# An encoder kernel: modulation sums turned into columns on TensorE, their weight tiles read by sixths and in another order

## The chip, the cores and the metric

The kernel runs on one core of a Trainium2 chip. The metric is the device time of one execution in microseconds (us). Three runs of the kernel before took 875.2, 884.22 and 884.54 us (median 884.22). The profiled execution took 870.41 us.

## The reference

The kernel computes a trunk of two residual layers over 256 tokens of width 1024, in float32. What matters here is the modulation: each layer takes six vectors of 1024 from a conditioning vector, and uses them at different places.

```python
c_act = jax.nn.silu(c)
for l in range(2):
    mod = c_act @ ada_w[l] + ada_b[l]           # (1024) @ (1024, 6144)
    sh1, sc1, g1, sh2, sc2, g2 = jnp.split(mod[:, None, :], 6, axis=-1)
    h = _rmsnorm(x, norm_mix_g[l]) * (1.0 + sc1) + sh1
    # l = 0: z = h @ even_w_in; gated linear recurrence + neighbourhood attention; mixed = [..] @ even_w_out
    # l = 1: z = h @ odd_w_in;  dilated attention + pooling;                      mixed = [..] @ odd_w_out
    x = x + g1 * mixed
    h = _rmsnorm(x, norm_ffn_g[l]) * (1.0 + sc2) + sh2
    x = x + g2 * _conv_ffn(h, ffn_w_up[l], ffn_conv_w[l], ffn_conv_b[l], ffn_w_down[l])
return _rmsnorm(x, final_norm_g)
```

## The kernel before

All activations are feature-major (128 partitions are features, 256 tokens are columns). Projection weights come in **units** of 128x2048 float32 (1 MB). Each unit is read by SyncE (SP) into one of four buffers `w_raw`, rounded by ScalarE (ACT) into `w_hi` (`split_hi`, L474), subtracted by VectorE (DVE) into `w_lo` (`split_lo`, L704), and used by TensorE (PE) in 48 matmuls (`three`, L1049). `w_hi` and `w_lo` have two buffers (SPLIT = 2): `w_hi` of unit n+2 waits until PE is done with unit n. There are 110 units, in order: EI (16, input projection of layer 0), EO (4, its output projection), UP0 (22) and DN0 (11) (feed-forward), OI (20), OO (4), UP1 (22), DN1 (11).

Beside these, DVE computes `c_act @ ada_w`. A tile of 128 rows (k) by 1024 columns (q) is read into one of two buffers `ada_raw`; DVE multiplies it by `cact[:, k]` and adds it into `mod_acc` (`add_tile`, L714). The partition sum that is left is made on PE: `mod_sum` (L1112) runs one matmul for each 128 columns, with a one-hot picker as the stationary operand and `mod_acc` as the moving one, so that group g lands in row g; DVE copies the rows out (`keep_mods`, L719), PE transposes them (`mod_turn`, L1119), and DVE adds the bias (`take_mods`, L724). The first 2048 columns of layer 0 are summed in eight tiles at the start (L771, L774). The other 80 tiles follow in the order k outside, q inside, so that a group of 2048 or 4096 columns is complete only at its end; `mod_acc` is cleared by POOL (GpSimd) before each group.

Every engine runs its own list in program order and waits on semaphores. Where the 80 tiles stand on DVE: 20 beside EI (one for each of units 0 to 7, two for each of 8 to 12, one for 13 and 14), 9 in the neighbourhood attention (after each odd step of `attend`, 16 steps), 3 in the recurrence after it, 16 beside the first 16 units of UP0, 24 beside OI (two for each of its first four units, then one), 8 in the dilated attention (odd steps from 3 on). POOL loads the tiles (`tile_in`, L391: it waits until the buffer's tile is used, then issues), except those in the two attentions, which SP loads (L364, L375). After its first 20 tiles POOL computes the gates of the recurrence (L421 to L431).

In `attend` PE computes the scores of step s (L1201 or L1318 and L1323), transposes those of step s-2 (L1178) and multiplies by the values for step s-3 (L1206, or L1330 and L1333); DVE adds the bias and takes the maximum (L848 or L858, L840, L841), ACT takes the exponential (L552) and copies the transposes out (L559).

`norm` on DVE takes the reciprocal (L735), then per feature block a product (L747) and, after ACT's rounding (L495), the rest `h_lo` (L754). The update of x after DN0 is eight instructions on DVE (L983); ACT squares them (L483), PE sums (L1101). In the last unit of DN0 `down_summed` already tells DVE which blocks of x can be updated.

Of the kernel before, what the change touches and what calls it, by code (L numbers as in the profile page):

```python
# [14 lines left out]
P = 128  # L15
# [25 lines left out]
ADA1, ADA2, ADA3, ADAS = 8, 40, 56, 88  # L41
# [13 lines left out]
C_PICK = C_EPS + 1  # L55
C_HMEAN = C_PICK + 63
# [24 lines left out]
def shape_constants():  # L81
# [32 lines left out]
    a[:, C_PICK + 31] = 1.0  # L114
# [5 lines left out]
def encoder(nc, x, c, ada_w, ada_b, norm_mix_g, norm_ffn_g, even_w_in, even_w_out, hgrn_lb_logits, hgrn_norm_g,  # L120
            na_rpb, odd_w_in, odd_w_out, pool_w, pool_scale, ffn_w_up, ffn_conv_w, ffn_conv_b, ffn_w_down,
            final_norm_g, consts_in, out):
    with ExitStack() as ctx:
# [31 lines left out]
        mod_rows = sb("mod_rows", [32, P])  # L155
# [80 lines left out]
        rest_landed = [sem(f"rest_landed{i}") for i in range(2)]  # L236
        ada_used, acc_zeroed, mod_summed, mod_ready = sem("ada_used"), sem("acc_zeroed"), sem("mod_summed"), sem("mod_ready")
# [20 lines left out]
        down_summed, mod_gathered, mod_kept = sem("down_summed"), sem("mod_gathered"), sem("mod_kept")  # L258
# [38 lines left out]
        def _(sp):  # L297
# [63 lines left out]
            for tile in range(20, 32):  # L361
                sp.wait_ge(ada_used, ADA1 + tile - 1)
                k, q, slot = tile // 4, tile % 4, tile % 2
                sp.dma_start(ada_raw[:, slot, :], ada_w[0, k * P:(k + 1) * P, 2048 + q * 1024:3072 + q * 1024]).then_inc(  # L364
                    rest_landed[slot], 16)
# [6 lines left out]
            for tile in range(24, 32):  # L372
                sp.wait_ge(ada_used, ADA3 + tile - 1)
                k, q, slot = (tile - 16) // 2, 2 + tile % 2, tile % 2
                sp.dma_start(ada_raw[:, slot, :], ada_w[1, k * P:(k + 1) * P, 2048 + q * 1024:3072 + q * 1024]).then_inc(  # L375
                    rest_landed[slot], 16)
# [9 lines left out]
        def _(pool):  # L386
            def tile_in(l, k, q, slot, i2, t2):

                pool.wait_ge(ada_used, i2 * 2 + 2 * t2 + slot - 1)
                src = ada_w[l].rearrange("(k p) n -> k p n", p=P)[bass.ds(k, 1), :, q:q + 1024]  # L390
                pool.dma_start(ada_raw[:, slot, :], src.rearrange("k p n -> p (k n)")).then_inc(ada_landed[slot], 16)  # L391

            def head(l, base):
                tile_in(l, 0, 0, 0, 0, base // 2)
                tile_in(l, 0, 1024, 1, 0, base // 2)
                with pool.Fori(1, KT) as k:
                    for q in (0, 1):
                        tile_in(l, k, q * 1024, q, k, base // 2)
# [289 lines left out]
        def _(dve):  # L688
# [18 lines left out]
            def add_tile(k, q, slot, i2, t2, landed=ada_landed, before=ADA1):  # L707

                dve.wait_ge(ada_used, i2 * 2 + 2 * t2 + slot - 1)
                if before == ADA1 and t2 >= ADA2 // 2:  # L710
                    before += 12
# [680 lines left out]
```

## Time and profile before

| | |
|---|---|
| profiled execution, its time | 870.41 us |
| its span (first to last instruction) | 868.7 us |
| median of three runs | 884.22 us (875.2 to 884.54) |
| TensorE busy | 797.4 us (92%) |
| VectorE busy | 599.5 us (69%) |
| ScalarE busy | 422.8 us (49%) |
| GpSimd busy | 71.7 us (8%) |
| DMA | 171.17 MB, mean 197 GB/s |

Times in the rows are microseconds from the span's start unless marked ns. Busy shares are averages over stages with different limits, so each stage is read by itself. "PE" is the matmul, "PEld" the load of its stationary operand, which overlaps it. An arrow "<-" after a time names what ended the idle time before it. "PEclk" is the clock that TensorE was granted: 1.00 is 2.4 GHz, 0.50 is 1.2 GHz.

### The profile page before, as it was taken

To read this page: it belongs to the slowest core of one execution; us is meant where nothing else is said; L and a number is where in the kernel's file an instruction comes from. 1 tells how busy PE (TensorE), PEld (TensorE's weight loads), DVE (VectorE), ACT (ScalarE), POOL (GpSimd) and SP (SyncE) were. 2 spreads that over 40 slices of the span, in tenths; PEclk is the share of its full clock that TensorE was granted. 3 is DMA by queue.
4 is the path that set the end of the run, shared out by engine and by line. 5 is a ranking of instruction groups with operands and counts; after the bars stand their busy time and mean duration, and the time that the engine had idled before them with its cause. 6 is when DMAs were issued, how large, how long until landed. Compare 5 with 4: busy or idle time off the path is not lost.

```text
span 868.7 us, 17243 instructions
## 1 busy us (share of the span) xinstructions
PE 797.4 (92%) x6580; PEld 750.3 (86%) x6580; DVE 599.5 (69%) x870; ACT 422.8 (49%) x664; POOL 71.7 (8%) x89
## 2 busy tenths in 40 slices
PE   3399998986898999999989999999998999999996
PEld 2299996675788999999979899977787999999995
DVE  3876687779759999874466766667735777776444
ACT  4244464331246666663345444634344666666332
POOL 0200117000200000000020100050000000000000
PEclk9699998577899999999999999995579999999998
DMA  9999885322364999755563898852505576765511
GB/s 360 332 261 330 295 287 194 98 73 81 116 175 122 289 289 290 221 198 207 185 224 134 296 308 296 279 170 76 144 3 146 144 194 193 193 194 194 193 49 48
DMA packets 160047, 171.17 MB, mean 197 GB/s; under 512 B 5178, under 2 KB 142339, under 8 KB 158979
## 3 DMA queue, kind: packets, MB, share of 16 engines
q1 hardware_dynamic: 151363, 139.11, 51.0%
q0 software_dynamic: 8640, 31.46, 10.2%
q8 instruction: 29, 0.48, 0.2%
q14 instruction: 15, 0.12, 0.0%
HBM read 169.50 MB, written 1.05 MB: 196 GB/s over the span
## 4 chain that ended last, share of the span: by engine, by line
PE 79%; DVE 12%; DMA 5%; issue 2%; ACT 1%; SPq 1%; POOLq 0%; DVEq 0%; ACTq 0%
PE acc L1049 50%; PE big L1049 14%; DMA ada_raw<-in_ada_w 4%; PE aux L1178 2%; DVE mod_acc L774 2%; DVE mod_acc L714 2%; DVE qk L287 2%; PE big L1318 2%; PE aux L1101 1%; PE big L1201 1%; PE acc L1206 1%; PE acc L1330 1%; DVE w_lo L704 1%; PE big L1323 1%; PE acc L1112 1%
## 5 line engine op out<-in xcount | busy, mean ns | idle before, releaser
L1049 PE MATMUL acc<-h_hi,w_hi 128*128 128x256 f32 x1248 | 351.4, 282 | 17.3 <-DVE h_lo L754 14.8
L1049 PE MATMUL acc<-h_lo,w_hi 128*128 128x256 f32 x1248 | 348.6, 279 | 0.0
L1049 PE MATMUL acc<-h_hi,w_lo 128*128 128x256 f32 x1248 | 348.6, 279 | 0.0
L704 DVE TENSOR_TENSOR w_lo<-w_raw,w_hi 128x1024 fp32r<-128x1024 f32 x220 | 263.1, 1221 | 105.0 <-ACT w_hi L474 104.9
L474 ACT ACTIVATE w_hi<-w_raw 128x1024 fp32r<-128x1024 f32 x220 | 224.5, 1050 | 101.3 <-PE big L1049 62.4
L1049 PEld LDWEIGHTS acc<-h_hi,w_hi 128*128 128x128 f32 x1248 | 238.4, 191 | 19.6 <-issue 17.7
L1049 PEld LDWEIGHTS acc<-h_lo,w_hi 128*128 128x128 f32 x1248 | 238.1, 191 | 0.4
L1049 PEld LDWEIGHTS acc<-h_hi,w_lo 128*128 128x128 f32 x1248 | 237.8, 191 | 0.0
L714 DVE SCALAR_TENSOR_TENSOR mod_acc<-ada_raw,cact,mod_acc 128x1024 f32<-128x1024 f32 x80 | 106.8, 1338 | 21.8 <-DMA ada_raw<-in_ada_w 21.6
L1049 PE MATMUL big<-hid_hi,w_hi 128*128 (+1 forms) x352 | 97.2, 276 | 0.0
L1049 PE MATMUL big<-hid_lo,w_hi 128*128 (+1 forms) x352 | 97.2, 276 | 0.0
L1049 PE MATMUL big<-hid_hi,w_lo 128*128 (+1 forms) x352 | 97.2, 276 | 0.0
L1049 PEld LDWEIGHTS big<-hid_hi,w_lo 128*128 128x128 f32 x352 | 66.1, 188 | 0.0
L1049 PEld LDWEIGHTS big<-hid_hi,w_hi 128*128 128x128 f32 x352 | 66.1, 188 | 0.0
L1049 PEld LDWEIGHTS big<-hid_lo,w_hi 128*128 128x128 f32 x352 | 66.1, 188 | 0.0
L391 POOL DMA_DIRECT2D ada_raw<-in_ada_w x60 | 32.1, 535 | 287.3 <-DVE mod_acc L714 287.3
L610 ACT ACTIVATE conv<-acc,vecs 128x256 f32<-128x256 f32 x44 | 24.9, 565 | 59.2 <-PE acc L1049 58.5
L952 DVE SCALAR_TENSOR_TENSOR conv<-acc,vecs,conv 128x255 f32<-128x255 f32 x44 | 21.2, 483 | 39.3 <-ACT conv L610 37.5
L1049 PE MATMUL acc<-w_hi,h_hi 128*128 128x256 f32 x144 | 40.0, 278 | 0.7 <-DVE w_lo L704 0.7
L1049 PE MATMUL acc<-w_hi,h_lo 128*128 128x256 f32 x144 | 39.8, 277 | 0.0
L1049 PE MATMUL acc<-w_lo,h_hi 128*128 128x256 f32 x144 | 39.8, 277 | 0.0
L523 ACT ACTIVATE ze<-acc 128x512 f32 (+1 forms) x16 | 9.6, 598 | 47.5 <-PE acc L1049 47.5
(184 smaller groups left out, 911.8 us busy)
## 6 DMA issues: line engine op xcount, KB each, us to landing
w_raw<-in_ffn_w_up SPq DMA_DIRECT2D x88, 512.0 KB, 5.0
ada_raw<-in_ada_w POOLq DMA_DIRECT2D x60, 512.0 KB, 5.6
w_raw<-in_ffn_w_down SPq DMA_DIRECT2D x44, 512.0 KB, 4.0
w_raw<-in_odd_w_in SPq DMA_DIRECT2D x40, 512.0 KB, 5.0
w_raw<-in_even_w_in SPq DMA_DIRECT2D x32, 512.0 KB, 6.0
ada_raw<-in_ada_w SPq DMA_DIRECT2D x20, 512.0 KB, 3.8
ada_first<-in_ada_w SPq DMA_DIRECT2D x5, 1024.0 KB, 8.1
w_raw<-in_even_w_out SPq DMA_DIRECT2D x8, 512.0 KB, 5.2
```

The lines of the kernel that those rows point to most:

```text
L287: return eng.tensor_tensor(to, to, total.unsqueeze(3).to_broadcast([P, 2, half // (2 * h), h]), ALU.mult)
L391: pool.dma_start(ada_raw[:, slot, :], src.rearrange("k p n -> p (k n)")).then_inc(ada_landed[slot], 16)
L474: nc.scalar.activation(w_hi[:, n % SPLIT, part], w_raw[:, n % RAW, part], ACT.Copy).then_inc(s_hi, 1)
L523: nc.scalar.activation(to, acc[:, (n - first) % 2, :], ACT.Copy, scale=scale).then_inc(z_evicted, 1)
L610: nc.scalar.activation(conv[:, a, :], acc[:, a, 0:T], ACT.Identity, bias=vecs[:, bass.ds(i * 4 + (V_CB + l * FT + u), 1)], scale=vecs[:, b ...
L704: dve.tensor_tensor(w_lo[:, n % SPLIT, part], w_raw[:, n % RAW, part], w_hi[:, n % SPLIT, part].bitcast(F32), ALU.subtract).then_inc(s_lo, 1)
L714: dve.scalar_tensor_tensor(out=sums, in0=ada_raw[:, slot, :], scalar=cact[:, bass.ds(k, 1)], in1=sums, op0=ALU.mult, op1=ALU.add).then_inc ...
L774: dve.scalar_tensor_tensor(out=sums, in0=ada_first[k], scalar=cact[:, k:k + 1], in1=sums, op0=ALU.mult, op1=ALU.add).then_inc(ada_used, 1)
L952: dve.scalar_tensor_tensor(out=conv[:, a, 1:T], in0=acc[:, a, 0:T - 1], scalar=tap(0), in1=conv[:, a, 1:T], op0=ALU.mult, op1=ALU.add).the ...
L1049: ins = pe.matmul(dst, lhsT, rhs, start=start and n == 0, stop=stop and n == 2, skip_group_check=True)
L1178: ins = pe.transpose(aux[:, r % 2, j * P:(j + 1) * P], (ns if base == 0 else cs)[:, r % 4, j * P:(j + 1) * P], ident)
L1318: pe.matmul(bank[:, 0:T], rows(0, 0, t * P, P), rows(6, 0, 0, T), start=True, stop=True)
```

## The change

`mod_sum`, `keep_mods` and `mod_turn` go, with the picker, `mod_rows` and the clearing of `mod_acc`. In their place PE takes `mod_acc` as the stationary operand and one column of ones as the moving one, once for each 128 columns, and DVE adds the bias to what stands in PSUM. The tiles are taken a sixth (1024 columns) at a time, all eight k of it, and each sixth is turned into columns shortly before its use. POOL loads all 80 tiles; its loops and DVE's are written out.

```diff
+ADA_FIRST = 8
+ADA_TILES = [(0, q, k) for q in (2, 3, 4, 5) for k in range(KT)] + [(1, q, k) for q in range(6) for k in range(KT)]
+ADA_AT = {(0, 2): 0, (0, 3): 1, (0, 4): 2, (0, 5): 3, (1, 0): 0, (1, 1): 1, (1, 2): 2, (1, 3): 3, (1, 4): 0, (1, 5): 1}
+def ada_summed(l, q):
+    return ADA_FIRST + ADA_TILES.index((l, q, KT - 1)) + 1
 ...
@@ sync: the loads of the tiles in both attentions go
-            for tile in range(20, 32):
-                sp.wait_ge(ada_used, ADA1 + tile - 1)
-                ...
-            for tile in range(24, 32):
-                ...
@@ gpsimd
+            def load_tiles(first, last):
+                for tile in range(first, last):
+                    l, q, k = ADA_TILES[tile]
+                    pool.wait_ge(ada_used, ADA_FIRST + tile - 1 if tile >= 2 else 6)
+                    pool.dma_start(ada_raw[:, tile % 2, :], ada_w[l, k * P:(k + 1) * P, q * 1024:(q + 1) * 1024]).then_inc(
+                        ada_landed[tile % 2], 16)
-            pool.wait_ge(mod_gathered, 1)
-            pool.memset(mod_acc[:], 0.0).then_inc(acc_zeroed, 1)
-            rest(0, ADA1, 0, 5)
+            load_tiles(0, 20)
             pool.wait_ge(lb_ready, 1)
 ...         (the gates, L421 to L428)
             pool.tensor_tensor(qk[:, 2, :], qT, fT[0], ALU.mult).then_inc(gates_ready, 1)
+            load_tiles(20, 22)
             pool.wait_ge(z_evicted, N_EI)
             pool.tensor_tensor(own_k, qk[:, 0, :], qk[:, 3, :], ALU.add).then_inc(own_ready, 1)
-            ...
+            load_tiles(22, 72)
 ...         (the pooling, L448 to L458)
+            load_tiles(72, 80)
@@ scalar
-                stream(act, first_down, N_DN, 4, lambda i, n: split_hi(i, n + SPLIT)) if l == 0 else \
-                    stream(act, first_down, N_DN - SPLIT, 4, lambda i, n: split_hi(i, n + SPLIT))
+                stream(act, first_down, N_DN - 1 if l == 0 else N_DN - SPLIT, 4, lambda i, n: split_hi(i, n + SPLIT))
 ...
             rms(2)
+            split_hi(0, OI + 1)
             norm(2, mods[:, 1, 0:8])
@@ vector
+            def add_tiles(first, last):
+                for tile in range(first, last):
+                    l, q, k = ADA_TILES[tile]
+                    sums = mod_acc[:, ADA_AT[l, q] * 1024:(ADA_AT[l, q] + 1) * 1024]
+                    dve.wait_ge(ada_landed[tile % 2], (tile // 2 + 1) * 16)
+                    if k == 0:
+                        dve.tensor_scalar(sums, ada_raw[:, tile % 2, :], cact[:, 0:1], None, ALU.mult).then_inc(ada_used, 1)
+                        continue
+                    dve.wait_ge(ada_used, ADA_FIRST + tile)
+                    dve.scalar_tensor_tensor(out=sums, in0=ada_raw[:, tile % 2, :], scalar=cact[:, k:k + 1], in1=sums,
+                                             op0=ALU.mult, op1=ALU.add).then_inc(ada_used, 1)
@@ norm: the fourth norm takes its shift and gain first
                 if idx:
                     reciprocal_rms(idx)
+                if idx == 3:
+                    take_mods(5, 1, 24, 16, aux[:, 1])
+                    make_gain(3, 1, 32, V_NFFN + KT)
@@ EI: the same places as before (20 tiles)
+            in_units(EI, EI + 8, 0, 1)
+            in_units(EI + 8, EI + 10, 8, 2)
 ...
@@ neighbourhood attention: 4 tiles, after steps 3, 7, 11, 15
-                if s < STEPS + 2 and s % 2:
-                    add_rest(20 + s // 2)
+                if s % 4 == 3 and s < STEPS:
+                    add_tiles(20 + s // 4, 21 + s // 4)
@@ recurrence: 3 tiles go
-            add_rest(29)
-            add_rest(30)
-            add_rest(31)
-            keep_mods(1, 32, big[:, 0])
+            take_mods(1, 0, 16, 24, big[:, 0])
@@ UP0 16 tiles, DN0 1 and then 2 for each unit, DN1; UP1 8 tiles
+                    for u in range(N_UP):
+                        up_step((24 + u, 25 + u) if u < 16 else (0, 0))(0, first_up + u)
+                    split_lo(0, first_down + SPLIT)
+                    add_tiles(40, 41)
+                    take_mods(2, 0, 40, 8, aux[:, 1])
+                    for u in range(1, N_DN - 1):
+                        split_lo(0, first_down + u + SPLIT)
+                        add_tiles(39 + 2 * u, 41 + 2 * u)
                 else:
+                    for u in range(N_UP):
+                        up_step((72 + u // 2, 73 + u // 2) if u < 16 and u % 2 else (0, 0))(0, first_up + u)
+                    split_lo(0, first_down + SPLIT)
+                    take_mods(6, 1, 40, 8, aux[:, 1])
+                    stream(dve, first_down + 1, N_DN - SPLIT - 1, 4, lambda i, n: split_lo(i, n + SPLIT))
@@ OI: 13 tiles, one for each of units 0 to 12
+            split_lo(0, OI + 1)
+            in_units(OI, OI + 13, 59, 1)
+            in_units(OI + 13, OI + N_OI, 72, 0)
@@ dilated attention: 8 tiles go; keep_mods and the second half of the rows go
-                if s == 2:
-                    keep_mods(3, 32, acc[:, 1])
 ...
+            take_mods(4, 1, 16, 8, aux[:, 1])
@@ tensor
+            def mod_columns(tiles, first, count, bank):
+                pe.wait_ge(ada_used, tiles)
+                for g in range(count):
+                    at0 = (first + g) % 32 * P
+                    ins = pe.matmul(bank[:, g:g + 1], mod_acc[:, at0:at0 + P], consts[:, C_ONE:C_ONE + 1], start=True,
+                                    stop=True)
+                ins.then_inc(mod_summed, 1)
+            mod_columns(ADA_FIRST, 0, 16, aux[:, 1])                           # before EI
+            mod_columns(ada_summed(0, 4), 0, 24, big[:, 0])                    # before EO
+                mod_columns(ada_summed(1, 4), 8 * ADA_AT[1, 3], 16, aux[:, 1]) # before UP1, after norm_sum_of(3)
+                mod_columns(ada_summed(l, 5), 8 * ADA_AT[l, 5], 8, aux[:, 1])  # between UP and DN, both layers
+            mod_columns(ada_summed(1, 1), 0, 16, aux[:, 1])                    # after DN0
+            mod_columns(ada_summed(1, 2), 8 * ADA_AT[1, 2], 8, aux[:, 1])      # before OO
-            attend(STEPS, ROW, dil_scores, dil_values, cpt, ctok, N_EI + N_OI, half_mods)
+            attend(STEPS, ROW, dil_scores, dil_values, cpt, ctok, N_EI + N_OI)
```

## Rows read from the trace of the kernel before

**Rows 1.** The page's busy digits in 40 slices of 21.7 us; PEclk is TensorE's granted clock.

```profile
PE   3399998986898999999989999999998999999996
PEclk9699998577899999999999999995579999999998
```

**Rows 2.** Table by stage: us, busy us and count of PE, PEld, DVE, ACT, POOL, clock, DMA.

```profile
138.00:182.00 44.00, 39.67 (x136) 27.18 (x134) 36.04 (x90) 17.09 (x57) 13.32 (x9) 0.56 0.34 104
572.00:634.00 62.00, 60.47 (x379) 44.20 (x377) 45.71 (x126) 25.54 (x61) 13.78 (x11) 0.62 0.36 103
```

**Rows 3.** Timeline of POOL after its first tiles: start, us, engine, line, operation.

```profile
143.56 2.35 POOL L428 TENSOR_TENSOR qk<-ze 128x1024 f32<-128x1024 f32 x1
145.87 3.33 POOL L429 TENSOR_TENSOR qk<-ze 128x1024 f32<-128x1024 f32 x1
```

**Rows 4.** Timeline of DVE in the neighbourhood attention: a tile, steps 4 and 16.

```profile
143.67 3.32 DVE L714 SCALAR_TENSOR_TENSOR mod_acc<-ada_raw,cact,mod_acc 128x1024 f32<-128x1024 f32 x1
146.91 0.15 DVE L829 RECIPROCAL stat<-stat 128x1 f32<-128x1 f32 x1
177.87 0.15 DVE L829 RECIPROCAL stat<-stat 128x1 f32<-128x1 f32 x1
```

**Rows 5.** Timeline around the first unit of EO.

```profile
222.12 7.17 PE L1112 MATMUL big<-mod_acc,consts 128*32 128x128 f32 x64
231.62 0.24 PE L1119 MATMUL big<-consts,mod_rows 32*128 32x32 f32 x1 [2.33 <-DVE mod_rows L719]
232.38 1.23 DVE L762 TENSOR_TENSOR h_lo<-work,h_hi 128x1024 fp32r<-128x1024 f32 x1 [0.81 <-ACT h_hi L590]
```

**Rows 6.** The chain of work that ended last: DN0, OI's first unit, OI's last 13 units.

```profile
384.97 59.85 PE big L1049 x528
...
457.32 7.33 PE acc L1049 x48
...
500.76 71.43 PE acc L1049 x624
```

**Rows 7.** Timeline of DVE after DN0: the updates of x, directly behind `w_lo`.

```profile
448.22 3.22 DVE L983 SCALAR_TENSOR_TENSOR xT<-big,mods,xT 128x256 f32<-128x256 f32 x8
```

**Rows 8.** Timeline of DVE in OI beside two tiles a unit.

```profile
471.69 2.36 DVE L704 TENSOR_TENSOR w_lo<-w_raw,w_hi 128x1024 fp32r<-128x1024 f32 x2 [0.62 <-ACT w_hi L474]
498.28 2.35 DVE L704 TENSOR_TENSOR w_lo<-w_raw,w_hi 128x1024 fp32r<-128x1024 f32 x2
```

**Rows 9.** DMA issues, KB each, median us to landing: tiles in UP0, weights in DN0.

```profile
ada_raw<-in_ada_w POOLq DMA_DIRECT2D x16, 512.0 KB, 6.3
w_raw<-in_ffn_w_down SPq DMA_DIRECT2D x12, 512.0 KB, 3.7
```

**Rows 10.** Timeline of weight loads and the sums, in the dilated attention.

```profile
575.16 3.68 PE L1112 MATMUL acc<-mod_acc,consts 128*32 128x128 f32 x32
580.54 0.52 PEld L1330 LDWEIGHTS acc<-zo,cpt 128*128 128x128 f32 x4
589.25 0.98 PEld L1330 LDWEIGHTS acc<-zo,cpt 128*128 128x128 f32 x4
```

**Rows 11.** Windows of 2 us (columns as in Rows 2) where the clock falls.

```profile
142.00:144.00 2.00, 0.20 (x1) 0.23 (x2) 1.86 (x7) 1.10 (x4) 1.92 (x3) 0.92 0.53 111
584.00:586.00 2.00, 1.55 (x15) 0.91 (x13) 1.90 (x9) 0.81 (x3) 1.84 (x3) 1.00 0.77 209
```

**Rows 12.** Timeline of PE: scores of steps 6 and 15, and what ends the stage.

```profile
587.17 1.03 PE L1318 MATMUL big<-zo 64*128 64x256 f32 x2
622.92 1.22 PE L1318 MATMUL big<-zo 64*128 64x256 f32 x2
633.99 3.64 PE L1351 MATMUL big<-pmean,poolw 128*128 128x256 f32 x8
```

**Rows 13.** Timeline of the norm before UP1: the last sums and DVE's reciprocal.

```profile
667.09 1.13 PE L1101 MATMUL aux<-squared,consts 128*128 128x256 f32 x4 [0.16 <-ACT squared L483]
668.76 1.75 DVE L735 RECIPROCAL rstd<-rstd 128x256 f32<-128x256 f32 x1 [1.79 <-ACT rstd L488]
```

More of the change, by code:

```diff
@@ L386, in _ @@
         def _(pool):
[L387 to L398, printed above, removed]
-            def rest(l, base, first=0, last=KT):
-                with pool.Fori(first, last) as k:
-                    for q in range(4):
-                        tile_in(l, k, 2048 + q * 1024, q % 2, k * 2, base // 2 + q // 2)
+            def load_tiles(first, last):
[4 more added lines that the diff above has]
+                        ada_landed[tile % 2], 16)
             done = [0]
@@ L785, in _, with in_units @@
             dve.tensor_tensor(lbt[:, 0, :], logits, logits, ALU.subtract).then_inc(lb_diff, 1)
-            dve.wait_ge(acc_zeroed, 1)
-            def in_step(first, base, tile0, per):
-                def step(i, n):
-                    if not (isinstance(i, int) and n + SPLIT in (EO, EO + 1, OO, OO + 1)):
-                        split_lo(i, n + SPLIT)
-                    for tile in range(tile0 + per * (n - first), tile0 + per * (n - first + 1)):
-                        add_tile(i * per + tile // 4, tile % 4, tile % 2, i * 2 * per, base // 2 + tile // 2)
-                return step
+            def in_units(first, last, tile, per):
+                for n in range(first, last):
+                    if n + SPLIT not in (EO, EO + 1, OO, OO + 1):
+                        split_lo(0, n + SPLIT)
+                    add_tiles(tile + per * (n - first), tile + per * (n - first + 1))
             def keep_bias(first, last):
@@ L1104, in norm_sum_of @@
                     ins.then_inc(norm_sum, 1)
-            def mod_sum(e, tiles, count, bank, first=0, last=None):
+            def mod_columns(tiles, first, count, bank):
                 pe.wait_ge(ada_used, tiles)
-                last = count if last is None else last
-                for g in range(first, last):
-                    pick = consts[:, C_PICK + 31 - g:C_PICK + 31 - g + count]
-                    ins = pe.matmul(bank[0:count, 0:P], pick, mod_acc[:, g * P:(g + 1) * P], start=g == first,
-                                    stop=g == last - 1)
-                ins.then_inc(mod_gathered, 1)
-            def mod_turn(e, count, bank):
-                pe.wait_ge(mod_kept, e + 1 + (e == 3))
-                pe.transpose(bank[:, P:P + count], mod_rows[0:count, :], ident[0:count, 0:count]).then_inc(mod_summed, 1)
+                for g in range(count):
[3 more added lines that the diff above has]
+                ins.then_inc(mod_summed, 1)
             pe.wait_ge(s_ident, 16)
```

111 lines of the change are left out of this document (14 added, 97 removed).

## The prediction

> **What bounds the kernel now.** I read the page's digits first. PE is busy nearly everywhere, but its granted clock falls in two places, slices 6 to 10 and 31 to 33 [rows 1]. The table by stage says which: the neighbourhood attention at a mean clock of 0.56 and the dilated attention at 0.62; elsewhere PE streams units at 59.85/11 = 5.44 us each [rows 2, 6]. So a change outside PE counts only where it makes PE wait, adds to PE's list, or moves the point at which the clock falls. The tiles do this in three ways: DVE is in program order, so a tile that has not landed holds back `w_lo` or a step of attention behind it; POOL loads tiles and computes, in order too; and DVE's tile time in the attentions opens gaps on PE. The sums at 222 to 229 are hidden beside the reciprocals of the recurrence; those after step 2 of the dilated attention are not.
>
> **Price of a column.** Before, 16 groups took 3.68 us at full clock [rows 10]. After, each is a full 128x128 weight load, recorded twice for float32, and one moving column. No row has one moving column. Nearest is L1330, 128x128 loads with 64 moving columns: four in 0.52 us, one every 0.11 after the first (0.19), and 0.98 at half clock, one every 0.21 [rows 10]. I take 0.22 us a group at full clock: 8 groups 1.75, 16 groups 3.5, 24 groups 5.3. The lower end is nothing at all, since a single moving column may need no wait for the load before; the upper is 0.43, both loads at half clock. So PSUM columns cost what rows cost; the gain is only the copy and the transpose.
>
> The Trainium skill, TensorE: Matmul & The Clock Gate, section Back-to-back issue gap, lists matmuls of 1 to 64 columns at about 60 cycles, a floor of about 25 ns. Read alone it would make 16 groups 0.8 us; an estimate by that page. Rival D below is what this would do here, priced from the rows.
>
> **Part by part**, each against the profiled execution (870.41 us, span 868.7; the median of the runs is 13.8 us above it).
>
> 1. *Start.* 16 groups at half clock cost at most 16 x 0.43 = 6.9 us instead of 6.3; copy and transpose (0.6) go. Zero, bounds +0.6 and -3. Clearing `mod_acc` is off the path. EI has its 20 tiles at the same places: zero.
>
> 2. *Neighbourhood attention: +6.5.* Nine tiles of 1.28 us become four, which gains nothing by itself: from step 4 at 146.91 to step 16 at 177.87 the cadence is 2.58 us and the mean clock is half [rows 2, 4]. But tile 20 changes queue. SP issued it before the stage began; now POOL issues it behind the gates. The last two products there start at 143.56 (2.35) and 145.87 (3.33 beside DVE's stretched tile; 2.35 without it), so the issue comes at 148.2 [rows 3]. It lands 3.7 us later at best (weights of the same size in the quieter DN0) and 6.3 at worst (tiles in UP0) [rows 9]; I take 4.2, as nothing else is read here. DVE wants this tile after step 3, at about 142.5, since the tile after step 1 is gone. It stands until 152.4, and step 4 starts at 153.7 instead of 146.91: +6.8, less 0.4 for the second stretched tile that goes. Behind that wait stand all steps, so PE idles about 8 us; the clock fell after a shorter gap (0.20 busy in 2 us [rows 11]) and stays down. Bounds +5.5 and +9.
>
>    That tile took 3.32 us and POOL's product 3.33 side by side [rows 3, 4]. The Trainium skill, SBUF — State Buffer, says that the port pair that VectorE and GpSimd share is an exclusive lock, against a VectorE instruction with two SBUF inputs too. By it the product takes 2.35 when DVE stands; without it the term would be 1 us larger.
>
> 3. *Recurrence and EO: -2.* Three tiles leave DVE where it had time. PE's 24 groups end at 222.1 + 5.3 = 227.4, and no transpose makes it wait for DVE until 231.62: the first half of EO's first unit (24 matmuls, 2.7 us) runs before `h_lo`, which ends at 233.6 [rows 5]. Gain 2.8 at full clock, 1 if the wait brings the clock down. I take 2.
>
> 4. *UP0.* 16 tiles as before, zero. Eight groups between UP0 and DN0, 1.75 us, are in the next sum.
>
> 5. *DN0: +7.* It had no tiles; now 19, two beside each unit from the second on. The row with two tiles a unit is OI's start: `w_lo` at 471.69 and, four units later, at 498.28, a cadence of 6.65 us against PE's 5.44 [rows 8]. A buffer's round is its use, POOL's issue and the landing. From DN0's start: PE ends unit 0 at 7.2, and `w_lo` of unit n+2 is done 3.4 to 3.5 after unit n (the last one ended at 448.2, PE at 444.8) [rows 6, 7]. Units 2 to 4 get theirs at 10.7, 16.1, 21.5, still by PE's pace; unit 5 at 27.3. Six cadences on, OI's first has it at 67.2, its two tiles end 4.3 later, less 1.2 as two tiles only multiply: 70.3. There the updates of x begin, where they began at 448.22 - 384.97 = 63.25. The moved `split` of OI's second unit (ACT 2 us, DVE 2.36) is in that difference; it now sits behind the norm, where ACT has the reciprocal's 1.75 us as cover and DVE ends it 0.2 us after PE needs it. Bounds: landings of 3.7 bring DVE's round under PE's pace and the updates to about 62 (-1); those of 6.3 in UP0 [rows 9] a cadence of 7.9 and 79 to 80 (+16).
>
> 6. *OI: -3.3.* Thirteen single tiles fit 5.44 us (2.36 + 1.28). Seven units took 500.76 - 457.32 = 43.4 us against 38.1; 1.9 of the excess is the first unit's (7.33), the rest goes [rows 6]. Bounds -4, -2.5.
>
> 7. *Dilated attention: -4.* 16 groups leave PE's list after step 2 (3.6), and DVE's tiles there, but the clock falls about as early. PE had been busy 1.55 of 2 us before step 6 at 587; from there steps take (622.92 - 587.17)/9 = 3.97 us [rows 11, 12]. DVE's tiles are gone, yet ACT's `split_hi` at step 4 (2 us) and DVE's `split_lo` at step 8 (2.36) remain, each a gap on PE. Bounds: -2.5, and rival A.
>
> 8. *Before OO: -1.* 8 groups for 16 and a transpose less, but PE then waits for `h_lo`, and the clock may rise later. Bounds +0.6, -2.3.
>
> 9. *Norm before UP1: +1.5.* 16 groups start at 668.2 and end 3.5 later, at 671.7; DVE's reciprocal ended at 670.5 and its products began. Bias and gain (0.4) come after: products at 672.1, +1.6. PE is idle less, and the clock may hold: bounds 0, +1.9 [rows 13].
>
> 10. *UP1 to DN1: +1.75*; the 8 tiles of UP1 fit as UP0's 16 do.
>
> Sum: 0 + 6.5 - 2 + 7 - 3.3 - 4 - 1 + 1.5 + 1.75 = **+6.5 us**: 876.9 against the profiled execution, 890.7 against the median. The four times of before lie at 870.4, 875.2, 884.2 and 884.5, and nothing here says which kind of execution comes next; I put the time between these two, nearer the median: 886.
>
> **Rivals.**
>
> *A: the clock holds in the dilated attention* (0.25). Half of 3.97 is 1.99; with handovers that don't scale I take 2.4 us a step. Steps 6 to 15 gain 1.6 each (16), the last part, 622.92 to 633.99, gives 5, and the two splits cost 5: term 7 is -20. Term 8, now at full clock, is -3. Total -11.5, faster. For it: PE at full clock up to 586 even beside tiles and POOL; against: the splits, one of which ran when the clock fell. If it holds only to step 9, the total is +1.
>
> *B: DN0 is paced by landings* (0.2). Beyond a cadence of 7.0 us the kernel is over 1% slower. A landing of 5.3 makes it 7.2 and the total +10.5; the 6.3 of UP0 makes it 7.9 and the total +16. For: 2 MB a unit on the DMA engines, twice what DN0 had. Against: weights in DN0 land in 3.7, half that of tiles in UP0 [rows 9].
>
> *C: tile 20 is not late* (0.1): POOL lets it out before the gates end, or DVE comes later. Then no gap at 143: total 0, or -10 if the clock also stays up.
>
> *D: a group costs nothing but its issue* (0.1): terms 9 and 10 and 1.75 of term 5 go, total +2.
>
> *The forecast* has 0.35.
>
> A measurement of this kernel can tell about 1% (8.8 us) from no change. Faster by over 1%: A in most of its share, half of C: 0.23. Slower by over 1%: B, and the forecast with its DN0 term above 9: 0.32. The rest 0.45. Range: A on a quick execution is 859, on the median 872.7; B on the median 895 to 900. I leave out the outer parts: 866 to 900. The forecast's own range is 874 to 895.
>
> **What would show it.** DVE idle 8 to 11 us before a tile after step 3, released by the DMA; `w_lo` every 6.65 us in DN0 and PE waiting for it; the updates of x 70 us after DN0's start; no wait for tiles in OI; the clock's fall at step 5 to 8 of the dilated attention; groups of 0.22 us. I am wrong if tile 20 lands before 146, if DN0 stays at 60 to 62 us, or if the clock stays up past step 12.

## The result, and the profile after

The kernel after takes 919.93 us (median of 4 runs, 915.35 to 921.37) against 879.71 (4 runs beside it): a ratio of 1.053, with a 95% interval of 1.045 to 1.062. It is slower by some 40 us, where I had forecast 886 us with 900 as the upper end. The profiled executions stand at 920.08 and 870.41 us.

The table by stage of the kernel after, first for the neighbourhood attention, then for the stretch that holds the start of the dilated attention (columns as in [rows 2]; line numbers are those of the kernel after):

```profile
141.00:191.00 50.00, 39.37 (x134) 26.89 (x132) 26.62 (x85) 16.46 (x56) 15.07 (x15) 0.52 0.23 71
604.00:606.00 2.00, 2.00 (x17) 1.19 (x15) 0.36 (x2) 1.45 (x2) 0.33 (x1) 1.00 0.00 0
606.00:608.00 2.00, 1.53 (x19) 0.93 (x18) 1.90 (x9) 1.62 (x3) 1.85 (x3) 0.91 0.00 0
608.00:610.00 2.00, 1.99 (x6) 1.01 (x6) 1.93 (x6) 0.71 (x2) 1.92 (x2) 0.50 0.00 0
```

Then the chain of waits of the kernel after: start, us, what. These are the long pieces of PE, in the order of EI, UP0, OI, UP1, and the last two with the columns of the modulation before them.

```profile
41.27 59.22 PE acc L994 x480
...
270.36 129.66 PE acc L994 x1056
...
487.11 117.39 PE acc L994 x960
...
709.64 128.62 PE acc L994 x1056
...
838.26 1.68 PE aux L1056 x16
839.95 63.46 PE big L994 x528
```

The last row is the one to read. DN1 has no tiles, no waits and no edit but the columns ahead of it; its 528 matmuls are those of [rows 6], where DN0 took 59.85 us (DN1 took 59.84). Now they take 63.46. UP0 went from 121.45 us to 129.66 for 1,056 matmuls, and UP1 from 121.54 to 128.62. Streamed matmuls have become slower in stages that the change doesn't touch. The timeline shows it one by one (start, us, engine, line):

```profile
290.06 0.28 PE L994 MATMUL acc<-h_hi,w_hi 128*128 128x256 f32 x1
290.18 0.28 PE L994 MATMUL acc<-h_lo,w_hi 128*128 128x256 f32 x1
290.30 0.28 PE L994 MATMUL acc<-h_hi,w_lo 128*128 128x256 f32 x1
290.42 0.28 PE L994 MATMUL acc<-h_hi,w_hi 128*128 128x256 f32 x1
290.54 0.28 PE L994 MATMUL acc<-h_lo,w_hi 128*128 128x256 f32 x1
```

One start every 0.12 us. I took the distances between the starts of all matmuls of this kind (5,280 in each kernel; those of 108 to 130 ns, over 5,100 of them, which leaves out waits, changes of stage and the stretches at half clock) and found three values and little else: in before 113.3 ns, and 117.8 in some stretches; in after 120.0 ns, always. The mean above 113.33 ns, times 5,280, I call the **pace's part**: 2.4 us in before, 35.1 in after. Without it the spans are 866.3 and 883.2 us: +16.9. So some 33 of the 49.6 us are a pace that no term of the prediction contains, and 17 stand against the predicted 6.5. The split is an estimate: it takes PE to be the limit everywhere, which it isn't in DN0 (below), and it holds against the profiled execution of before, a quick one with one matmul in ten at 117.8.

What the change does to the layout is easy to miss in the diff. The picks in the constants shrink from 63 columns to one and `mod_rows` goes: 704 bytes less. Buffers are placed one behind another, so `h_hi`, `h_lo` and the arena (with `hid_hi`, `hid_lo`) move down by 704 bytes in each partition, while `w_hi` and `w_lo` stay. From `w_hi` to `h_hi` it is 88 KiB and 704 bytes in before, 88 KiB exactly in after.

### The profile page after: what moved, and what is told of

Its sections match the earlier page's. It is cut to its first block, busy times and chain, and to the rows that moved or that the text cites. A ratio compares the mean times of both kernels' runs of the same rounds, so it can differ in the third digit from the quotient of the medians.

```text
span 918.3 us, 16610 instructions
## 1 busy us (share of the span) xinstructions
PE 842.4 (92%) x6576; PEld 797.4 (87%) x6576; DVE 589.9 (64%) x868; ACT 422.4 (46%) x664; POOL 68.8 (7%) x106
## 4 chain that ended last, share of the span: by engine, by line
PE 80%; DVE 8%; DMA 6%; issue 2%; ACT 2%; POOL 1%; SPq 1%; DVEq 0%; ACTq 0%; POOLq 0%
PE acc L994 55%; PE big L994 8%; DMA ada_raw<-in_ada_w 5%; PE aux L1116 2%; PE aux L1056 2%; DVE mod_acc L749 2%; DVE qk L291 2%; PE big L1258 2%; PE aux L1046 2%; DVE mod_acc L690 1%; PE acc L1270 1%; PE big L1139 1%; PE acc L1144 1%; PE big L1263 1%; PE big L1056 1%
## 5 line engine op out<-in xcount | busy, mean ns | idle before, releaser
L994 PE MATMUL acc<-h_hi,w_hi 128*128 128x256 f32 x1248 | 361.3, 289 | 13.2 <-DVE h_lo L729 13.2
L994 PE MATMUL acc<-h_lo,w_hi 128*128 128x256 f32 x1248 | 359.0, 288 | 0.0
L994 PE MATMUL acc<-h_hi,w_lo 128*128 128x256 f32 x1248 | 358.6, 287 | 0.0
L447 ACT ACTIVATE w_hi<-w_raw 128x1024 fp32r<-128x1024 f32 x220 | 224.2, 1049 | 114.4 <-PE big L994 71.7
L994 PEld LDWEIGHTS acc<-h_hi,w_hi 128*128 128x128 f32 x1248 | 245.8, 197 | 14.4 <-issue 14.0
L994 PEld LDWEIGHTS acc<-h_lo,w_hi 128*128 128x128 f32 x1248 | 245.8, 197 | 0.4
L994 PEld LDWEIGHTS acc<-h_hi,w_lo 128*128 128x128 f32 x1248 | 245.6, 197 | 0.0
L690 DVE SCALAR_TENSOR_TENSOR mod_acc<-ada_raw,cact,mod_acc 128x1024 f32<-128x1024 f32 x70 | 89.7, 1281 | 37.3 <-DMA ada_raw<-in_ada_w 36.6
L994 PE MATMUL big<-hid_hi,w_hi 128*128 (+1 forms) x352 | 100.2, 285 | 3.2 <-DVE w_lo L677 3.2
L386 POOL DMA_DIRECT2D ada_raw<-in_ada_w x80 | 42.8, 535 | 662.5 <-DVE mod_acc L690 346.1
L915 DVE SCALAR_TENSOR_TENSOR conv<-acc,vecs,conv 128x255 f32<-128x255 f32 x44 | 21.2, 483 | 50.7 <-ACT conv L583 50.7
L1056 PEld LDWEIGHTS aux<-consts,mod_acc 128*128 128x128 f32 x144 | 22.0, 241 | 13.2 <-DVE mod_acc L749 12.9
```

What stands on the lines that cost most here:

```text
L386: pool.dma_start(ada_raw[:, tile % 2, :], ada_w[l, k * P:(k + 1) * P, q * 1024:(q + 1) * 1024]).then_inc(ada_landed[tile % 2], 16)
L447: nc.scalar.activation(w_hi[:, n % SPLIT, part], w_raw[:, n % RAW, part], ACT.Copy).then_inc(s_hi, 1)
L690: dve.scalar_tensor_tensor(out=sums, in0=ada_raw[:, tile % 2, :], scalar=cact[:, k:k + 1], in1=sums, op0=ALU.mult, op1=ALU.add).then_inc(a ...
L915: dve.scalar_tensor_tensor(out=conv[:, a, 1:T], in0=acc[:, a, 0:T - 1], scalar=tap(0), in1=conv[:, a, 1:T], op0=ALU.mult, op1=ALU.add).the ...
L994: ins = pe.matmul(dst, lhsT, rhs, start=start and n == 0, stop=stop and n == 2, skip_group_check=True)
L1056: ins = pe.matmul(bank[:, g:g + 1], mod_acc[:, at0:at0 + P], consts[:, C_ONE:C_ONE + 1], start=True, stop=True)
```

## The experiments

**First group: the layout, and the late tile.** pad704 puts back the lost 704 bytes and keeps the change.

```diff
+        place[0] += 704
         h_at = place[0]
```

> The changed kernel with 704 bytes left free ahead of h_hi, so that h_hi, h_lo and all that follows stand at the addresses they have in the kernel before (the shorter constants and the missing mod_rows had moved them down by 704 bytes). Nothing else differs. Placement theory (the stationary and the moving operand's addresses set the pace of float32r matmuls): 48 matmuls of a unit take 5.44 to 5.5 us again instead of 5.77 to 5.9, the 110 units save 36 us, time about 883 us. Code theory (written-out loops, instruction reads or the mix on other engines slow PE): pace stays at 0.120 us a matmul, 919 us.

Measured: 893.45 us (4 runs), 1.012 [1.006, 1.019] of before; the profiled span 896.9. Some stages are at 113.3 ns, others at 117.8, none at 120.0. That is 26 us off the 919.93 of after, and 10 us above the 883 that I expected: the stretches at 117.8 were in no expectation of mine.

before320 does the reverse: the kernel before, with 320 bytes more ahead of `h_hi`, which makes the distance 89 KiB exactly.

> The kernel before with 320 bytes left free ahead of h_hi, so that h_hi has the same place within 1024 bytes as in the changed kernel. Placement theory: units slow from 5.44 to 5.77 us, +36 us, about 906 to 916 us. Code theory: 870 to 884 us as before.

Measured: 900.27 us (2 runs), 1.021 [1.013, 1.030] of before. Nothing of the change is in it, and its pace is 120.0 ns throughout. From its chain:

```profile
822.59 63.36 PE big L1050 x528
```

That shows that the layout alone does it, and that it does not need the change. The median is 20 us above that of before beside it (880.04), and not the 26 to 36 that were expected: the profiled execution of before had few stretches at 117.8, and others at its distance have more (below). So against medians the layout explains 20 to 26 of the 40 us, and 33 of 49.6 only against the quick profiled execution. pad64 is after with 64 bytes more.

> The changed kernel with h_hi and all behind it 64 bytes higher. If the place within 128 bytes decides (before: 64, after: 0, and w_hi and w_lo at 0), the pace is 0.113 us a matmul and the time about 883 us. If the place within 256 bytes or more decides, or only the exact address before is good, it stays near 919 us. Code theory: 919 us.

Measured: 906.2 us (1 run); 113.3 or 117.8 ns by stretches, mostly the latter: neither 883 nor 919.

pad704_early is pad704 with `load_tiles(0, 22)` ahead of POOL's gates, and no `load_tiles(20, 22)` behind them.

> As pad704, and POOL loads tiles 20 and 21 before it computes the gates. Queue theory (DVE's 9.6 us wait after step 3 is POOL's order): the wait for the DMA goes, step 4 starts some 7 to 9 us earlier, against pad704 -8 us, and up to -15 if the clock then holds longer. Rival (the stage is bound by PE at half clock and something else is late next, ACT or POOL's gates themselves): under 3 us.

Measured: 878.6 and 891.9 us; the trace is that of the first. Its timeline of POOL has the request ahead of the gates, and DVE waits 0.22 us for the tile after step 3 where after has 9.63:

```profile
135.61 0.53 POOL L387 DMA_DIRECT2D ada_raw<-in_ada_w  x1 [0.95 <-DVE mod_acc L690]
136.27 3.01 POOL L404 TENSOR_SCALAR ze<-ze,lbt 128x512 f32<-128x512 f32 x4
```

```profile
141.63 1.28 DVE L690 SCALAR_TENSOR_TENSOR mod_acc<-ada_raw,cact,mod_acc 128x1024 f32<-128x1024 f32 x1 [0.22 <-DMA ada_raw<-in_ada_w]
```

EO starts at 224.4 us where pad704 has 235.7. Of these 11.3 us, 8.6 are in the attention itself (42.1 us from EI's last matmul to the first one of the recurrence, for 50.7), 1.0 in EI, which the edit doesn't touch, and 1.7 between the attention and EO.

**Second group: which property of the layout.** The parts are h against w, h alone, the bytes moved, and the unit.

```diff
-        place = [(nc.sbuf_base + 63) // 64 * 64]
+        place = [(nc.sbuf_base + 63) // 64 * 64 + 64]   # base64, base64_h64
...
+        place[0] += 64                                   # base64_h64 (pad128: 128, pad32: 32)
         h_at = place[0]
```

> The kernel after, with h_hi, h_lo and all behind them moved up by 128 bytes (h_hi at byte 139520 of a partition, 0 modulo 128, like w_hi at 49280). Theory, parity: the pace of a float32r matmul hangs on whether the addresses of h and of w stand in the same half of a 128-byte line. Here they do again, as in after and before320, so all 5,280 matmuls go at 120.0 ns and the profiled span is 915 to 920 us (883 and the pace's 35). Rival, distance: what counts is how near the layout is to that of before (pad64 906, pad704 893): then 128 bytes give at most what 64 gave, some 903 to 908 us, at a mean of 117 to 118 ns.

> The kernel after, with every buffer, w_hi and w_lo too, moved up by 64 bytes (w_hi at 49344, h_hi at 139456, both 64 modulo 128). Theory, relative: w and h in the same half of a 128-byte line means 120.0 ns throughout, 915 to 920 us. Rival, absolute: it is the place of h alone that counts; with h at 64 modulo 128 the pace is 113.3 or 117.8 ns by stretches as in pad64, 890 to 907 us.

> The kernel after, with every buffer moved up by 64 bytes and h_hi, h_lo and all behind them by another 64 (w_hi at 49344, 64 modulo 128; h_hi at 139520, 0 modulo 128). Theory, relative: w and h stand in different halves of a 128-byte line, so 113.3 or 117.8 ns by stretches, 890 to 907 us. Rival, absolute: h at 0 modulo 128 means 120.0 ns throughout, 915 to 920 us.

> The kernel after, with h_hi, h_lo and all behind them moved up by 32 bytes (h_hi at 139424, 32 modulo 128; w_hi at 49280, 0 modulo 128). If the unit is a half line of 64 bytes, h still begins in w's half: 120.0 ns, 915 to 920 us. If each 32 bytes counts, the pace is another one: 113.3 ns throughout would give 883 to 888 us, and a value between gives 895 to 907 us.

Measured, one run each: 912.12, 920.11, 907.39 and 900.00 us. base64 goes at 120.0 ns throughout and base64_h64 at 113.3 or 117.8: the distance between the two operands decides, not the place of h. pad128 is at 118.7 and pad32 at 117.1 ns, so both of my rules failed: neither "half lines of 128 bytes" (which wanted 120.0 for both) nor "the nearer to before the better". Only the loosest expectation, a value between the two for pad32, was met.

**Third group: what is left without the pace.** spread is pad704 with the later tiles one to a unit:

```diff
+                    tile = 41
                     for u in range(1, N_DN - 1):
                         split_lo(0, first_down + u + SPLIT)
-                        add_tiles(39 + 2 * u, 41 + 2 * u)
+                        more = 2 if u in (2, 5) else 1
+                        add_tiles(tile, tile + more)
+                        tile += more
...
-            in_units(OI, OI + 13, 59, 1)
-            in_units(OI + 13, OI + N_OI, 72, 0)
+            in_units(OI, OI + N_OI, 52, 1)
```

> The kernel pad704 with one edit: in the first down projection DVE adds tiles 40 to 51 (one with each unit, two with units 2 and 5) and not 40 to 56 or so with two in each unit; tiles 52 to 71 go one with each unit of the odd input projection. Theory, landings: the chain of pad704 shows a wait for ada_raw of 4.2 to 6.8 us in each unit of that projection, with two tiles to a unit. With one tile it is the matmuls (48 by 113.3 ns, 5.44 us a unit) again, so the stage from its columns to the first matmul of the odd input projection takes 74 to 77 us where pad704 takes 86, and the span less the pace's part is 872 to 876 (pad704: 884.5). Rival, something else paces it (the w_down landing, a DVE that has three more things to do): 83 us or more in the stage and 881 to 885 in all.

> pad704 with both edits: tiles 20 and 21 are requested by POOL before the gates (as in pad704_early) and the later tiles are spread (as in spread). Theory: the two gains are in different stages and add up. pad704_early has 871.1 us less the pace's part, spread takes another 9 to 11 off: 860 to 863, and with a pace's part of 5 to 12 a span of 866 to 875, 868 to 878 us: equal to the kernel before or 1% faster. Rival, the gain of one stage is lost in the next (the odd input projection with 20 tiles takes 3 to 5 us more): 873 to 882, not faster than before.

> early_spread with 32 matmuls of the identity by itself (128x128, into an unused part of two banks) in steps 0 and 1 of the dilated attention, where the kernel before had the 32 matmuls that sum the modulation; the result of them is not used. Theory, clock: the work that left these steps had kept the clock at full, which fell 3.3 us into the stage in after and about 15 us into it in before; with the fill it falls 8 us or more later, the steps until then run at full clock and win back what the fill costs (3.5 us): the stage takes 68 to 70.5 us, as without it. Rival: the fall has nothing to do with what PE does in these steps; it comes as early, and the stage takes 3.5 us more, 72 to 73 us.

> The kernel after with h_hi, h_lo and all behind them moved up by 96 bytes (h_hi 96 bytes above w_hi, modulo 256). Runs so far, by the distance from w_hi to h_hi modulo 256: 0 bytes 120.0 ns, 32 bytes 117.1, 64 bytes 113.3 or 117.8 by stretches, 128 bytes 118.7, 192 bytes 113.3 or 117.8 by stretches. Theory, a smooth function with its floor between 64 and 192 is already against the 128 bytes; by a rule of half lines 96 bytes lies as 64 and 32 together: 115 to 117.8 ns, a span of 893 to 906 us. Rival: 96 gives 113.3 throughout, 883 to 887 us.

spread: 889.3 us. DN0 from its columns to OI's first matmul takes 78.8 us, 76.4 without the pace's part; pad704 has 86.3 and 85.8. The whole gained less: the span without the pace's part is 881.2, for 884.5 of pad704, and 872 to 876 had been expected. The dilated attention gave back 3.5 us (71.9 for 68.4, from OI's last matmul to OO's first), beside a clock that was down for 71.7 us and not 61.4; why it was is not shown. For DN0 the chain of waits says why. This is DN0 in the kernel after, a round of which is a landing, an addition and an issue:

```profile
418.37 5.36 DMA ada_raw<-in_ada_w
423.73 0.02 issue
423.75 1.30 DVE mod_acc L690
425.05 0.28 issue
425.33 4.17 DMA ada_raw<-in_ada_w
429.50 0.02 issue
429.53 1.30 DVE mod_acc L690
430.82 0.28 issue
431.11 6.47 DMA ada_raw<-in_ada_w
...
467.09 6.01 DMA ada_raw<-in_ada_w
```

and this is DN0 in spread, where the DMA is gone from the chain and PE is one piece:

```profile
391.29 62.30 PE big L997 x528
```

early_spread: 875.3 us (872.97 to 878.55), 0.9948 [0.9904, 0.9992] of before. Span 876.8, pace's part 14.1, the rest 862.7, in the range that was expected.

early_spread_fill: 881.22 us, 1.0001 [0.9966, 1.0035]. The 32 records of the sums [rows 10] are 16 matmuls, each recorded twice, so my 32 matmuls were twice what I had meant: 7.5 us of PE, not 3.5.

```profile
571.11 3.84 PE L1282 MATMUL aux<-consts 128*128 128x128 f32 x32
574.88 0.70 PE L1260 MATMUL big<-zo 64*128 64x256 f32 x2
```

Its clock in windows (columns as in [rows 2]) is first that of early_spread, then its own:

```profile
576.00:578.00 2.00, 1.37 (x13) 0.87 (x13) 1.93 (x8) 1.22 (x4) 1.92 (x2) 1.00 0.00 0
578.00:580.00 2.00, 0.70 (x10) 0.36 (x5) 1.90 (x7) 1.15 (x4) 1.84 (x3) 0.63 0.00 0
```

```profile
583.00:585.00 2.00, 1.36 (x10) 1.01 (x10) 1.15 (x5) 1.57 (x6) 2.00 (x2) 1.00 0.03 8
585.00:587.00 2.00, 2.00 (x16) 1.78 (x15) 1.36 (x4) 0.00 (x0) 1.07 (x2) 0.60 0.32 70
```

OI's last matmul is at 572.5 in the one and 569.9 in the other, and the clock falls 6.0 and 15.5 us behind it. So what PE does in steps 0 to 2 does move the fall, as expected, and to where before had it (571.9, fall at 587.4): before and before320 have it 15.5 and 15.1 us behind OI's last matmul, the kernels with neither sums nor fill 3.3 to 6.6. But the stage takes 75.1 us against 68.9: of the 7.5 us of fill only 1.3 come back. Neither number of the expectation was met (68 to 70.5 for the one theory, 72 to 73 for the other); scaled to a fill of half the size, the second was the nearer.

pad96: 916.34 us, 119.8 ns, outside both values expected of it.

**Fourth and fifth group: the period, and whether the pace belongs to the kernel.** All are early_spread with another number in the place of 704; early_spread_2 is early_spread itself, on another chip.

> early_spread with h_hi, h_lo and all behind them 512 bytes above their place in after in the place of 704: the distance from w_hi to h_hi is 88 KiB and 512 bytes. Theory, a pattern that repeats every 256 bytes (0 in after and 1 KiB further in before320 gave 120.0 ns, 64 and 704 gave 113.3 or 117.8): 512 is like 0, 120.0 ns throughout, 862.6 + 35 = 896 to 899 us. Rival, the pattern repeats every 1,024 bytes only: 512 gives another pace, 866 to 890 us.

> early_spread with 256 bytes in the place of 704. Theory, a pattern of 256 bytes: 120.0 ns throughout, 896 to 899 us. Rival, 512 or 1,024 bytes: another pace, 866 to 890 us.

> early_spread with 736 bytes in the place of 704, which is 224 modulo 256 and 96 modulo 128. By a pattern of 256 bytes that is the same on both sides of 0, it goes like 32: 117.1 ns, 880 to 884 us. By a pattern in which only the place within 128 bytes counts, it goes like 96: 119.8 ns, 895 to 899 us. By neither (113.3 throughout): 864 to 868 us, which would be the best place of all.

> early_spread with 832 bytes in the place of 704: 64 modulo 256, where 704 is 192. Pattern of 128 bytes in which an odd half line is what counts: 113.3 or 117.8 ns by stretches as with 704, 866 to 884 us. If 704 is better than 64 (115.7, 114.4, 114.5 and 116.0 ns in four kernels against 117.5 and 117.0 in two), this one goes at 117 to 117.8 nearly throughout: 880 to 887 us.

> The same kernel as early_spread, profiled again and timed in more rounds. Theory: the pace of 113.3 or 117.8 ns is taken anew in each execution whenever TensorE starts after a wait, so the stages that show 117.8 (both up projections and the first down projection the last time) are others this time, while the span less the pace's part stays at 860 to 866 us; the median is 872 to 878 us, 0.990 to 0.999 of before. Rival: the pattern of stages belongs to the kernel and its waits; the same stages show 117.8, and the span is 875 to 878 again.

> early_spread with 672 bytes in the place of 704 (160 modulo 256). By the runs so far, modulo 256: 0 gives 120.0 ns, 32 117.1, 64 113.3 or 117.8 by stretches, 96 119.8, 128 118.7, 192 113.3 or 117.8, 224 118.2. If only the odd multiples of 64 reach 113.3, this one has a fixed mixture of 116 to 120 ns: 878 to 898 us. If it is 113.3 throughout, 864 to 868 us, better than all others.

Measured: 898.99, 905.73, 892.43, 884.30, 881.27 (8 runs, 876.31 to 885.34) and 897.51 us. es_512 came as the period of 256 bytes wanted it; es_256 had its 120.0 ns but took 7 us more than that; es_736, at 118.2 ns, met none of its three values. es_832 has stretches at both paces, as the first theory wanted; es_672 lies in its range. All nineteen kernels in one table, by the distance from `w_hi` to `h_hi` modulo 256 bytes:

| distance | mean ns (kernel) | pace's part, us | span less that part |
|---|---|---|---|
| 0 | 120.0 (after) | 35.1 | 883.2 |
| 0 | 120.0 (base64) | 35.1 | 883.2 |
| 0 | 120.0 (before320) | 35.1 | 865.8 |
| 0 | 120.0 (es_512, es_256) | 35.1, 35.1 | 862.1, 868.8 |
| 32 | 117.1 (pad32) | 19.6 | 878.6 |
| 64 | 117.5, 117.0 (pad64, base64_h64) | 21.8, 19.3 | 882.6, 886.3 |
| 64 | 116.2 (es_832) | 15.3 | 867.1 |
| 96 | 119.8 (pad96) | 33.9 | 880.6 |
| 128 | 118.7 (pad128) | 28.2 | 882.1 |
| 160 | 118.2 (es_672) | 25.5 | 870.2 |
| 192 | 113.8 (before) | 2.4 | 866.3 |
| 192 | 115.7, 114.4, 114.5 (pad704, pad704_early, spread) | 12.4, 5.7, 6.3 | 884.5, 871.1, 881.2 |
| 192 | 116.0, 114.8 (early_spread, its second execution) | 14.1, 7.5 | 862.7, 869.5 |
| 192 | 115.5 (early_spread_fill) | 11.5 | 873.2 |
| 224 | 118.2 (es_736) | 25.7 | 864.9 |

Five kernels at 0 (88 KiB, 88 KiB and 256, 88 KiB and 512, and 89 KiB) go at 120.0: the pattern repeats every 256 bytes, as far as these show. (In UP1 of es_256 the starts are uneven, 117 to 124 ns apart, with the same mean of 120.0.) Only 64 and 192 hold 113.3 for a stretch. At 32, 96, 128, 160 and 224 the starts are unevenly spaced, with means between.

Whether a long stretch at 192 goes at 113.3 or 117.8 is not fixed by the kernel. Here is the chain of early_spread in UP0, UP1 and DN1, and that of its second execution:

```profile
257.83 126.07 PE acc L996 x1056
...
673.96 126.20 PE acc L996 x1056
801.84 59.95 PE big L996 x528
```

```profile
261.54 121.53 PE acc L996 x1056
...
675.25 122.84 PE acc L996 x1056
...
799.77 62.30 PE big L996 x528
```

Three of the long stages have changed places, in the same program: 126.07 and 121.53, 126.20 and 122.84, 59.95 and 62.30. Where a pace changes in the traces, PE had mostly waited, its clock had just risen, or the kind of unit had changed (features or tokens in rows); within a stretch it stays. That other stages would show 117.8 was what I expected; that the rest would stay at 860 to 866 us (869.5) and the median at 872 to 878 (881.27) was not met. Three things keep this short of a draw in each execution. The two executions were on two chips, so the chip may be what differs. Not all stages change: OI goes at 113.3 for over four fifths of its matmuls in all seven traces at 192, that of before among them. And the pace is not all of the scatter: after, whose trace has 120.0 throughout, spreads over 6.0 us in four runs. The difference bounds what the timing can say: with up to 4.7 us in each up projection, the kernel before itself had medians of 873 to 882 us in the six sets of runs. early_spread came out at 0.9948 [0.9904, 0.9992] on one chip and at 1.0081 [1.0044, 1.0118] on another. Each interval excludes no change, to opposite sides, so no version here is shown to be better than before; this one equals it within some 1%.

## Why the prediction was wrong

**The step that failed is one that it didn't have.** It took PE's pace in every unit from before (5.44 us, "PE's 5.44" in terms 5 and 6) and carried it over to a kernel whose operands lie elsewhere. That is some 33 of the 49.6 us between the profiled executions: the runs showed 120.0 ns a matmul, 5.76 us a unit, in its place, and before320 showed it with nothing of the change in the kernel. Nothing in the trace of before could have priced it, but its range should have: the diff takes away two things that stand ahead of `h_hi`, and "placement changes" is a rival that can be read off it.

Point by point, with the pace's part taken out of both kernels (chains and timelines of the two, stage starts at the first streamed matmul):

| term | predicted | measured | where |
|---|---|---|---|
| 1, 2 start, neighbourhood attention | +6.5 | +5.0 | ends at 191.0 for 182.2, less 3.8 |
| 3 recurrence, EO | -2 | -3.1 | 79.4 us for 81.3, less 1.2 |
| 4 UP0 | 0 | +1.2 | 129.66 for 121.45, less 7.0 |
| 5 DN0 | +7 | +11.2 | 87.1 us for 72.35, less 3.5 |
| 6 OI | -3.3 | -3.2 | 117.3 for 114.8, less 5.7 |
| 7 dilated attention | -4 | +0.2 | 69.7 for 69.5 |
| 8, 9 OO, norm | +0.5 | +3.8 | 35.5 for 30.7, less 1.0 |
| 10 UP1 to DN1 | +1.75 | +1.8 | 130.3 for 121.54, less 7.0 |
| DN1 to the end | 0 | 0.0 | 78.3 us for 74.8, less 3.5 |
| sum | +6.5 | +16.9 | |

Each row compares one execution with one. base64, which has the code and the pace of after, differs from it by 1.6 us in the neighbourhood attention and by 1.9 from there to EO.

*Term 2* was right in its wait; its size is in part luck. DVE stands before the tile after step 3, released by the DMA, from 145.3 to 154.92; POOL issues at 150.60 and the landing takes 4.3:

```profile
148.32 2.34 POOL L411 TENSOR_TENSOR qk<-ze 128x1024 f32<-128x1024 f32 x1
150.60 1.15 POOL L386 DMA_DIRECT2D ada_raw<-in_ada_w  x2
```

```profile
154.92 1.28 DVE L690 SCALAR_TENSOR_TENSOR mod_acc<-ada_raw,cact,mod_acc 128x1024 f32<-128x1024 f32 x1 [9.63 <-DMA ada_raw<-in_ada_w]
```

The product beside a standing DVE takes 2.34 us, where it took 3.33 beside a tile [rows 3]. The Trainium skill, SBUF — State Buffer, section Who interferes with whom, says that a VectorE instruction with two SBUF inputs contends with a GpSimd instruction that reads SBUF; the trace agrees. From EI's last matmul to the first one of the recurrence the attention takes 44.2 us in before, 50.7 in after and 42.1 in pad704_early. So the wait costs 8.6 us, where I had 6.8, and the rest of the change, five tiles fewer, gains 2.1, where I had nothing; the two errors cancel to my +6.5. Rival C, no wait, was worth more than its 0 to the total for the same reason: -2 and not 0 in this stage.

*Term 5* was the mis-sized one. I had a cadence of 6.65 us, read in OI, and the last tiles right behind the last `w_lo`. The chain shows a round of landing, 1.30 and 0.30: from 418.37 to 467.09 seven rounds, 6.96 us each, with landings of 4.17 to 6.47. The last one is waited for as well:

```profile
473.13 2.67 DVE L690 SCALAR_TENSOR_TENSOR mod_acc<-ada_raw,cact,mod_acc 128x1024 f32<-128x1024 f32 x2 [3.30 <-DMA ada_raw<-in_ada_w]
```

So the updates of x begin 75.7 us after UP0's end and not 70.3, and from them to OI it is 11.4 us for 9.1. This is rival B in all but its threshold, a cadence beyond 7.0; it priced a landing of 5.3, and the median in DN0 is 5.4. I had given it 0.2. I had weighed its "against" by the weights' 3.7 us, but in DN0 these take 4.2 (median) and POOL's tiles 5.4. spread settles that it is the tiles and not `w_down` alone: with one tile to a unit 9.4 us go. The +11.2 is a lower value, as the 3.5 us of pace that it leaves out are mostly hidden behind the landings: pad704, with 0.5 us of it, still has 85.8 us here, which is +13.4 (one execution each).

*Terms 7 and 8* assumed that the clock would fall about as early, counted from the steps. It fell 3.4 us after OI's last matmul, where it had stayed up for 15.5: the 3.7 us of sums after step 2 [rows 10] had been part of what kept PE busy. With them gone PE waits for the first exponentials, and the clock is down for 71.7 us and not 51.2. The timeline has the wait and, behind it, the first scores at half clock:

```profile
606.45 0.70 PE L1258 MATMUL big<-zo 64*128 64x256 f32 x2
607.07 0.46 PE L1263 MATMUL big<-zo 64*64 64x64 f32 x8
608.01 0.90 PE L1116 MATMUL aux<-consts,cs 128*128 128x128 f32 x3 [0.49 <-ACT cs L525]
608.85 1.22 PE L1258 MATMUL big<-zo 64*128 64x256 f32 x2
```

The work saved was paid back at half clock, and the starts of the scores say where. Counted from OI's last matmul, step 3 has them at 7.3 us in before and at 4.6 in after, step 6 at 15.3 and 16.2: steps 3 to 5 lose all that the sums had gained. From step 6 to step 15 it is 35.7 and 35.9 us, so the tiles that left DVE there gained nothing; at half clock these steps are PE's. The fill of early_spread_fill says the same from the other side: a later fall is bought with PE's time, and little of it comes back. The clock also rises late: in after PE is still at half clock in the first 5 us of OO, which is some 2 of the 3.8 us there (an estimate).

```profile
676.00:679.00 3.00, 3.00 (x16) 3.00 (x15) 0.00 (x0) 0.00 (x0) 0.00 (x0) 0.50 0.00 0
```

*The price of a column* stood. Eight groups took 1.68 us at full clock (0.21 each, 105 ns for each of the 16 records; I had 0.22), so rival D falls. The Trainium skill, TensorE: Matmul & The Clock Gate, section Back-to-back issue gap, gives an issue floor of some 25 ns for so few columns; the trace has four times that. The same section says that in a stream of weight loads and matmuls both set the spacing.

*Term 9* came as +1.9, its upper bound, from the last of the norm's sums to the first matmul of UP1, with the products at 707.83 behind the columns. So term 8 is the other +1.9, where I had -1.

## What to carry to other kernels

A change that adds or removes a buffer moves every buffer behind it. Before timing such a change, pad the gap so that the distance between the operands of the hot matmuls stays what it was, and compare a stage that the change doesn't touch in both traces: if DN1 has moved, the rest of the comparison can't be read yet. And where a DMA with two buffers is added to a stage, cost its round (landing, use, issue) with landings read from a stage in which both queues are busy.

## What the runs showed of the hardware

- The pace of float32r matmuls of 256 columns, each with its own weight load, at full clock hangs on where the moving and the stationary operand lie to each other: 120.0 ns at a distance of a multiple of 256 bytes, 113.3 or 117.8 at 64 and 192, means of 117.1 to 119.8 at the other multiples of 32. At 2.4 GHz the first three are 288, 272 and 282.7 cycles. The Trainium skill, TensorE: Matmul & The Clock Gate, section Back-to-back issue gap, gives 262 cycles for 256 columns (109.2 ns, an estimate by that page) as the isolated gap, without a budget for the weight loads. No stream here reaches that figure. The Trainium skill, SBUF — State Buffer, section Who interferes with whom, calls the read ports of the two operands independent. A pace that depends on both addresses together is not what that leads one to expect; why it does is not shown.
- At half clock the distance costs nothing: the same matmuls go every 213 to 214 ns in all twenty traces, some 256 cycles at 1.2 GHz for 256 columns. This is after, at the distance that costs most at full clock:

```profile
237.65 0.41 PE L994 MATMUL acc<-h_hi,w_lo 128*128 128x256 f32 x1
237.86 0.41 PE L994 MATMUL acc<-h_hi,w_hi 128*128 128x256 f32 x1
238.08 0.41 PE L994 MATMUL acc<-h_lo,w_hi 128*128 128x256 f32 x1
```

- At 64 and 192 bytes a stretch gets one of two paces and keeps it, and two executions of one program, on two chips, differ in three of the long stages. What decides it stays open, and so does whether some distance that isn't a multiple of 32 is free of it; neither was tried.
- The scatter of the last column of the table (862.1 to 870.2 for the six kernels with both edits that differ in a pad alone, 878.6 to 886.3 for the eight without them) is too wide for one execution each to show anything smaller. Part of it is the length of the stretch at half clock in the dilated attention, 61.4 us in early_spread and 71.7 in spread; the cause of that difference is not shown.
